# A mixture-of-experts layer on one core: the down product of a block one block later, up in one pass, and three waits placed anew

## What is computed

```python
hn = rmsnorm(h, g_ffn).reshape(B * L, D)
y = h + hier_moe(hn, ...).reshape(B, L, D)      # then the final rmsnorm

# hier_moe: the best of 4 groups, in it the best 2 of 4 experts, 16 experts in all
def expert_block(args):
    xb_i, e = args
    h = jax.nn.silu(xb_i @ w_gate[e]) * (xb_i @ w_up[e])
    return h @ w_down[e]
```

## Time and profile before

| | |
|---|---|
| Median of 3 runs | 1982.25 us (1982.22 to 1984.65) |
| Profiled execution | 1982.03 us |
| Its span, first to last instruction | 1980.3 us |
| Mean granted TensorE clock over the span | 0.972 of full speed |
| TensorE busy in the span | 95% |
| Start of the first x transposes of phase three | 1208.0 us |

### The profile page before, as it was taken

The page is one execution under the profiler, slowest core; times in us unless marked ns, Lnnn a source line. Parts: engine busy times, 40 slices in busy tenths (PEclk is TensorE's granted clock), DMA queues, the critical chain, the costliest instruction groups (busy, mean ns, idle before and its releaser), DMA issues. The chain is left out here.

```text
span 1980.3 us, 29050 instructions
## 1 busy us (share of the span) xinstructions
PE 1882.3 (95%) x10232; PEld 1606.3 (81%) x10233; DVE 1061.0 (54%) x2070; ACT 735.3 (37%) x1393; POOL 414.7 (21%) x571
## 2 busy tenths in 40 slices
PE   7899999999999999999999955999999999999996
PEld 5899987788888788888888844888888888888885
DVE  5634343545444554455453335566677666665572
ACT  4332323333334333333333213444455444444351
POOL 2000000000201001000001014444444434434453
PEclk9899999999999999999999956999999999999998
DMA  6222233422335223333222425577678857655552
GB/s 226 87 86 86 86 131 107 155 85 86 98 137 201 76 95 98 127 128 107 88 100 90 170 87 196 193 284 254 224 249 291 295 202 256 222 198 200 193 178 92
DMA packets 166568, 309.98 MB, mean 157 GB/s; under 512 B 18448, under 2 KB 85008, under 8 KB 166490
## 3 DMA queue, kind: packets, MB, share of 16 engines
q1 hardware_dynamic: 133706, 223.61, 32.8%
q0 software_dynamic: 32784, 85.33, 12.4%
HBM read 256.13 MB, written 83.69 MB: 172 GB/s over the span
## 5 line engine op out<-in xcount | busy, mean ns | idle before, releaser
L64 PE MATMUL bank<-xT_hi,wh 128*128 128x512 f32 (+1 forms) x960 | 339.8, 354 | 7.3 <-ACT S L751 5.4
L65 PE MATMUL bank<-xT_lo,wh 128*128 128x512 f32 (+1 forms) x960 | 339.1, 353 | 0.0
L66 PE MATMUL bank<-xT_hi,wl 128*128 128x512 f32 (+1 forms) x960 | 338.2, 352 | 0.0
L799 DVE TENSOR_TENSOR wl<-raw,wh 128x512 fp32r<-128x512 f32 x352 | 219.5, 685 | 201.3 <-ACT wh L602 201.2
L1783 PE MATMUL bank<-gu_hi,ex_hi 128*128 128x256 f32 (+1 forms) x960 | 314.1, 327 | 5.0 <-DVE ex_lo L1655 4.7
L1784 PE MATMUL bank<-gu_lo,ex_hi 128*128 128x256 f32 (+1 forms) x960 | 306.7, 319 | 0.0
L1785 PE MATMUL bank<-gu_hi,ex_lo 128*128 128x256 f32 (+1 forms) x960 | 306.6, 319 | 0.0
L602 ACT ACTIVATE wh<-raw 128x512 fp32r<-128x512 f32 x352 | 192.4, 620 | 84.6 <-PE bank L1223 54.7
L64 PEld LDWEIGHTS bank<-xT_hi,wh 128*128 128x128 f32 x960 | 181.5, 189 | 36.0 <-issue 9.8
L1783 PEld LDWEIGHTS bank<-gu_hi,ex_hi 128*128 128x128 f32 x960 | 182.8, 190 | 28.7 <-DVE gu_lo L1655 5.9
L66 PEld LDWEIGHTS bank<-xT_hi,wl 128*128 128x128 f32 x960 | 181.6, 189 | 25.3
(11 more groups left out here) (239 smaller groups left out, 3258.3 us busy)
## 6 DMA issues: line engine op xcount, KB each, us to landing
raw<-in_w_in SPq DMA_DIRECT2D x56, 1024.0 KB, 5.1
raw_gate_up<-in_w_gate SPq DMA_DIRECT2D x16, 2048.0 KB, 8.2
raw_gate_up<-in_w_up SPq DMA_DIRECT2D x16, 2048.0 KB, 10.1
raw_d<-in_w_down SPq DMA_DIRECT2D x16, 2048.0 KB, 9.9
raw<-in_w_out SPq DMA_DIRECT2D x16, 1024.0 KB, 6.3
raw<-in_w_up_pool SPq DMA_DIRECT2D x16, 512.0 KB, 3.5
raw<-in_w_up_gmlp SPq DMA_DIRECT2D x16, 512.0 KB, 4.5
h<-in_x_prompt SPq DMA_DIRECT2D x16, 512.0 KB, 5.0
```

The lines of the kernel that those rows point to most:

```text
L64: nc.tensor.matmul(out, lh, rh, start=(i == 0), stop=False)
L65: nc.tensor.matmul(out, lh, rl, start=False, stop=False)
L66: last = nc.tensor.matmul(out, ll, rh, start=False, stop=(i == n - 1))
L799: lo = lambda out, x, hi: tt(out, x, hi.bitcast(F32), ALU.subtract)
```

## The change

- On TensorE block j runs gate, up in one pass of 512 columns into one bank, the x transposes of the next block, then down of block j-1, then all four hidden transposes of block j into one bank. Block 0 has no down, and down of the last block stands behind the loops.
- In an expert's second block TensorE waits for the whole split of the down weights. ScalarE starts that split only when down of the expert before has ended (`y_done`), and both engines do it at the end of the first block.
- ScalarE copies hT_hi, and VectorE writes hT_lo, each in one instruction of 512 columns, at the head of the next block.
- VectorE writes the next rows' low parts directly behind `hid`, and `scale` comes behind them, in all blocks.
- `add` is one block later in the count and waits, besides, until the z stored before it has landed (`z_out`). GpSimd copies idx_y ahead of its own wait for `z_out`, so `scale` doesn't wait for the store.
- GpSimd carries the indices one step longer: one more copy per step (idx_1 to idx_2). At the end there is one more round of addition, root, h gather, scale and output store.

```diff
-    bankG, bankU, bankY = psum[0], psum[1:3], psum[3:5]
-    bankX, bankH = psum[5:7], [psum[7], psum[0]]
+    bankG, bankU, bankY = psum[0], psum[1], psum[3:5]
+    bankX, bankH = psum[5:7], psum[7]
...
                     wait_apart(pool, x_tr, j, passed_pool)
+                    nc.gpsimd.tensor_copy(idx_2[:, :], idx_1[:, :]).then_inc(moved_2, 1)
+                    wait_apart(pool, moved_2, j, passed_pool)
                     nc.gpsimd.tensor_copy(idx_1[:, :], idx[:, :]).then_inc(moved, 1)
...
                     out_landed(j)
-                    wait_apart(pool, z_out, 16 * j, passed_pool)
                     nc.gpsimd.tensor_copy(idx_y[:, :], idx_z[:, :]).then_inc(moved_y, 1)
                     wait_apart(pool, moved_y, j, passed_pool)
+                    wait_apart(pool, z_out, 16 * j, passed_pool)
...
+                def hidden_high(j):
+                    act.wait_ge(th_done, j + 2)
+                    nc.scalar.activation(hT[0][:, :, :], bankH[:, :].rearrange("p (k i) -> p k i", k=KH),
+                                         ACT.Copy).then_inc(hT_hi, 1)
...
                 def per_block(e, i, lo, j, first=False):
+                    hidden_high(j - 1)
                     if not first:
                         use_sigmoid_table(0)
                         square(j + 1)
                     act.wait_ge(g_done, j + 1)
                     nc.scalar.activation(sg[:, :], bankG[:, :], ACT.Sigmoid).then_inc(sg_ok, 1)
+                    rows_high(j + 2)
                     if first:
+                        act.wait_ge(down_in, 16 * i + 16)
+                        act.wait_ge(y_done, lo + 2)
+                        for k in range(KH):
+                            nc.scalar.activation(dn[0][:, k, :], raw_d[:, k, :], ACT.Copy).then_inc(e_hi, 1)
...
-                def add(n):
+                def add(n, stored):
 
                     dve.wait_ge(y_done, n)
                     dve.wait_ge(final_ok, n)
+                    if stored is not None:
+                        dve.wait_ge(z_out, 16 * stored)
                     dve.wait_ge(h_rows_in, 16 * n)
...
                     if not first:
+                        add(j + 1, j)
+                    hidden_low(j - 1)
+                    mean(j + 1)
                     dve.wait_ge(sg_ok, j + 1)
                     tt(sg[:, :], bankG[:, :], sg[:, :], ALU.mult)
                     dve.drain()
+                    dve.wait_ge(gu_done, j + 2)
+                    tt(hid[:, :], bankU[:, :], sg[:, :], ALU.mult).then_inc(hid_ok, 1)
+                    rows_low(2 * j + 3)
+                    scale(j + 1)
                     if first:
+                        for k in range(KH):
+                            dve.wait_ge(e_hi, SPLITS_ACT * i + 2 * KD + k)
+                            lo_half(dn[1][:, k, :], raw_d[:, k, :], dn[0][:, k, :]).then_inc(e_lo, 1)
...
+                def down(j):
+                    pe.wait_ge(z_ok, 2 * j + 4)
+                    pe.wait_ge(hT_lo, j + 2)
+                    for k in range(KH):
+                        for half in range(2):
+                            last = accumulate(bankY[half][:, :], hT, k, dn, k, slice(half * HALF, (half + 1) * HALF),
+                                              k, KH)
+                    last.then_inc(y_done, 1)
...
                     for k in range(KD):
                         pe.wait_ge(e_lo, SPLITS * i + KD + k + 1)
+                        last = accumulate(bankU[:, :], xT, k, gu, KD + k, slice(0, HALF), k, KD)
                     last.then_inc(gu_done, 1)
                     rows_of_x(16 * j + 32)
+                    if not first:
+                        pe.wait_ge(e_lo, SPLITS * i + SPLITS)
+                    if not begin:
+                        down(j - 1)
+                    hidden_transposed(j)
```

More of the change, by code:

```diff
@@ L1402, in phase_three @@
         idx_1 = sb("idx_1", [P, FIELDS], I32)
+        idx_2 = sb("idx_2", [P, FIELDS], I32)
         idx_h = sb("idx_h", [P, FIELDS], I32)
@@ L1486, in _ @@
                 nc.gpsimd.memset(half_neg[:, :], -0.5).then_inc(spare_ok, 1)
[L1487 to L1490, removed]
+                for tile in (idx_1, idx_h):
+                    nc.gpsimd.iota(tile[:, 0:1], pattern=[[0, 1]], base=SEQ + SAMPLE, channel_multiplier=1)\
+                        .then_inc(spare_ok, 1)
+                    nc.gpsimd.memset(tile[:, 1:2], 0).then_inc(spare_ok, 1)
+                    nc.gpsimd.memset(tile[:, 2:3], NOWHERE).then_inc(spare_ok, 1)
                 nc.gpsimd.memset(idx_y[:, :], NOWHERE).then_inc(spare_ok, 1)
@@ L1573, in _ @@
                 store_final(total)
[L1574 to L1579, removed]
+                for last, n in ((False, total + 1), (True, total + 2)):
+                    out_landed(n)
+                    wait_apart(pool, z_ok, 2 * n, passed_pool)
+                    nc.gpsimd.tensor_copy(idx_y[:, :], idx_h[:, :]).then_inc(moved_y, 1)
+                    root(n)
+                    wait_apart(pool, moved_y, n, passed_pool)
+                    if not last:
+                        next_h(n + 1, idx_1)
+                    store_final(n)
                 wait_apart(pool, x_rows_in, 16 * total + 16, passed_pool)
-                out_landed(total + 2)
+                out_landed(total + 3)
             @block.scalar
             def _(act):
-                act.wait_ge(spare_ok, 8)
+                act.wait_ge(spare_ok, 11)
                 act.wait_ge(tab_ok, 1)
@@ L1720, in split, with hidden_low @@
                         lo_half(gu[1][:, k, :], raw_gu[:, k, :], gu[0][:, k, :]).then_inc(e_lo, 1)
-                def hidden_low(c):
-                    lo_half(hT[1][:, 2 * c:2 * c + 2, :], bankH[c][:, 0:2 * P].rearrange("p (k i) -> p k i", k=2),
-                            hT[0][:, 2 * c:2 * c + 2, :]).then_inc(hT_lo, 1)
+                def hidden_low(j):
+                    dve.wait_ge(hT_hi, j + 2)
+                    lo_half(hT[1][:, :, :], bankH[:, :].rearrange("p (k i) -> p k i", k=KH), hT[0][:, :, :])\
+                        .then_inc(hT_lo, 1)
                 def per_block(e, i, lo, j, first=False):
-                    def down(k):
-                        if first:
-                            dve.wait_ge(e_hi, SPLITS_ACT * i + 2 * KD + k)
-                            lo_half(dn[1][:, k, :], raw_d[:, k, :], dn[0][:, k, :]).then_inc(e_lo, 1)
                     if not first:
-                        add(j + 1)
-                        mean(j + 1)
+                        add(j + 1, j)
+                    hidden_low(j - 1)
+                    mean(j + 1)
                     dve.wait_ge(sg_ok, j + 1)
@@ L1763, in _ @@
                 total = dve.value_load(blk_tab[0:1, 2 * NE - 1:2 * NE], min_val=1, max_val=MAXBLK)
-                add(total + 1)
-                mean(total + 1)
-                scale(total + 1)
+                hidden_low(total - 1)
+                for n in (total + 1, total + 2):
+                    add(n, total)
+                    mean(n)
+                    scale(n)
             @block.tensor
```

100 lines of the change are left out of this document (20 added, 80 removed).

## The result

The changed kernel takes 2040.11 us in the median of 4 runs (2038.14 to 2042.7), against 1983.45 us (1982.22 to 1985.8) for the kernel before: ratio 1.0287, 95% interval 1.0274 to 1.0299. It is 2.9% slower, where 1966 was forecast. The profiled execution took 2042.7 us, with a span of 2040.6 us and a mean granted clock of 0.955 (before 0.972).

A forecast was written before the change was run, and what follows sets the result against it. TensorE's work was taken to bound plain blocks, level with VectorE's weight splitting at expert changes. Blocks -38.5, gather waits +13 and ends +9.6 gave -15.9 us from 1982.03: forecast 1966 us, range 1951 to 1989.

The forecast's parts named there:

- A plain block: TensorE's block without a change of expert: 18.01 us becomes 17.70, bounds 17.6 and 17.9.
- An expert change: TensorE's block at a change of expert: no stall on the split weights, 17.85 us each, for 15 changes.
- The split's cast: VectorE's split of the weights at an expert change: starts 4.8 us after the x transposes, bounds 4.8 and 6.1.
- rival 2: At expert changes VectorE's split starts 6.1 us after the x transposes, 0.9 more for each of 15: 1980 us; chance 0.12.
- the sum: TensorE's stretch of 39 blocks, without the gather waits and the ends: 688.9 us against 727.4, 38.5 gained.
- The ends: First block and the added down, addition and output round after the last block: 9.6 us more in all.
- the term for the gather: TensorE's waits for x at experts' second blocks, gather beside the raw_d reload: 4 x 2.5 + 10 x 0.3 = 13 us.
- rival 3: The reload starves every gather: 3 us in up to 14 second blocks, 25 to 42 instead of 13, 1978 to 1995; chance 0.22.
- "fresh" experts: Experts whose GpSimd chain isn't late: store of z 7.6 us, gather 0.7 us ahead of the reload, wait 0.3 us.
- chained experts: Experts after a two-block one, GpSimd's chain late: gather starts 12.9 us after the first block's x transposes, wait 2.5 us.
- the sign of being wrong: At second blocks: the prediction is wrong if the x transposes wait in the experts with no late GpSimd chain too.
- Rival 1: The gather's packets pass beside the reload and no block waits: -38.5 + 9.6, so 1953 us; chance 0.20.

The follow-up runs named there:

- the best version: The changed kernel with GpSimd's gather of x ahead of its wait for the stored z, and the reload held until the needed gather landed: 1953.26 us, ratio 0.9844.

## Why the prediction was wrong

**Right.** A plain block was forecast at 17.70 and is 17.69 to 17.70. Up runs at 0.227 a matmul in one pass. The first interval is 14.06 (14.0). An expert change with no wait ahead of it is 17.73 (17.85). The split's cast at the change near 1850.71 starts 4.53 behind x-tr, where I chose +4.8 between 4.8 and 6.1; rival 2 didn't come:

```profile
1855.24 0.43 DVE L1713 CAST gu_hi<-raw_gate_up 128x512 fp32r<-128x512 f32 x1 [0.35 <-issue]
```

The reload starts at T+12.37 (T+12.4). The 39 blocks without waits and slow clock take 686.8, and in the best version 686.44, against the 688.9 of the sum. The last output is issued 24.5 behind the last x-tr (24), and the one TensorE wait on z_ok stands there, not in the loops:

```profile
2015.21 0.49 PE L1770 MATMUL bank<-dn_hi,hT_hi 128*128 128x512 f32 x1 [2.81 <-DVE z_rows L1698]
...
2029.99 0.98 POOL L1532 DMA_INDIRECT out<-final_rows,idx_y  x1 [0.30 <-issue]
```

The ends cost 13.0 instead of 9.6: 10.8 of it behind the last x-tr (9.9). The rest lies ahead of the first marked one, which comes anywhere from 1228.5 to 1232.7 in the kernels of this case; that part says nothing of the change.

**Wrong: the term for the gather, 13 us against 60.9 and 27.0.** The place was right, and the number of waits was that of rival 3 (up to 14). Three steps failed: the price of a gather, the ten experts without a real wait, and the clock that a wait costs.

First, the price of a gather beside the reload. I took 7.4 us from the earlier trace rows as if any gather in the reload's way cost that. But that gather started 3.9 us behind the reload's issue, and mine was to start 0.5 behind it. The reload of the earlier trace rows took 11.8 us to land, so the whole of this gather ran beside it. Its row stands first here. The second, which the prediction left out too, is the gather of another expert, 5.3 us behind its reload (1893.04 against 1887.74):

```profile
raw_d<-in_w_down SPq DMA_DIRECT2D x1, 2048.0 KB, 11.8
...
x_rows<-hn_rows,idx POOLq DMA_INDIRECT x1, 5.4
```

In the kernel before a gather takes less, give or take 0.3 us, the later it starts behind the reload: 7.4 us at 3.9, 6.7 at 4.5, 5.4 at 5.3, 4.7 at 6.4. Twelve of them started from T+9.4 to T+11.9 and all landed between T+16.2 and T+17.1. So 7.4 is no price for a start beside the reload's issue; it had to be more. In the changed kernel the 14 started from 0.3 ahead of the reload to 1.6 behind it, took 7.7 to 9.1 us, and landed at T+21.0 to T+22.6. I had T+20.3. They don't simply land with the reload either: in the changed kernel they land between 2.1 us ahead of it and 0.2 behind, in the kernel before between 0.5 ahead and 2.1 behind. Landings as far behind the reload's issue as the twelve (10.7 to 11.5 us) would have given T+23.1 to T+23.9. What sets the time exactly stays open.

Second, the "fresh" experts. I gave ten of 14 a wait of 0.3, since a store of 7.6 us would put their gather at T+11.7, 0.7 ahead of the reload. The difference was real in the kernel before: the store of z took 6.8 to 7.7 us after a three-block expert, 8.7 to 9.6 after a two-block one. In the changed kernel it took 9.0 to 9.6 in all 14. The load of up that runs beside it took 8.4 to 9.3 us in the fresh experts before and takes 11.7 to 13.0 in all 14 now; why, no run tells. The gathers started at T+12.0 to T+14.0, and the two at T+12.0, 0.3 ahead of the reload, still took 9.0. They are both in chained experts, so fresh ones were no better off. A margin of 0.7 us on worked-out times carried ten of the 14 terms. This was the sign of being wrong that I had named. Nor did the waits alternate: I had TensorE's delay let GpSimd catch up, but the store of z started at T-2.5 to T-0.4 in each of the 14.

Third, a wait costs more than its length. The sum had no term for the clock behind a standstill, and that is 27.0 us here.

The start that I worked out for a chained expert fits the expert at 1808.29, though it follows a three-block one and was fresh by my terms: the store at T-0.4 (T-0.7), its landing at T+8.7 (T+8.1), the gather 4.5 behind that (4.8), so T+13.2 (T+12.9). Two sums of the prediction are a little off, with no weight: T+20.3 less T+17.7 is 2.6, not 2.5, and the four parts of the later end of down(last) add up to 7.35, not 7.1.

**Rivals.** Rival 3 named the mechanism and put it at 25 to 42 us; with the wait as measured it is 14 x 4.4 = 62, and with the 27 of the clock 89. Rival 1's number, 1953, is that of the version with the early gather and the held reload, 1953.26, but not by its mechanism: there the gathers don't pass beside the reload, they land before it starts.

The Trainium skill, "DMA: Bandwidth & Descriptors" (Queues, rings and completion order), lets each DMA engine take turns between its queues by the packet. By that rule I had estimated 8.8 us for a late gather; the trace has 8.9 for the one shown and 7.7 to 9.1 for all 14, so for a gather that overlaps the load from its start the rule agrees. It was the better price of the two.

## What to carry to other kernels

When a change moves a large load, don't price a small transfer beside it by one that was seen at another distance from the load's start: 8.9 us at 0.8 behind it, 7.4 at 3.9, 4.7 at 6.4. A saving on the bounding engine is safe only if the inputs of its next step arrive earlier too: here the blocks got 1 us shorter, and the gather landed 5 us later behind T. Long entries in the list of waits on engines with slack (46.3 and 22.3 us here) may be worth 4 us, and a new wait of 4.4 us on the bounding engine may cost 6.3.

## What the runs showed of the hardware

- A 512 KB gather takes about twice its time beside a 2 MB load. Started 1.1 us ahead of the load it takes 4.4 to 5.1 us; 0.3 ahead or level, 8.9 to 9.0; 0.84 behind, 8.9; 3.9 behind, 7.4; 6.4 behind, 4.7. Another load of 2 MB (gate, 0.63 ahead of the gather) gives 9.1.
- Behind a standstill of 4.3 us TensorE, busy throughout, had a granted clock of 0.59 for 6.6 us, and of 1.00 after that. Behind the 13 others it was 0.54 to 0.79 over the same length. The 14 standstills cost 27.0 us on top of their 60.9. With matmuls in the gap the clock behind it was 1.00.
- Three copies of 128 x 3 integers on GpSimd, 0.2 us each elsewhere, took 0.93, 0.97 and 0.69 us while VectorE subtracted 128 x 1024 tiles (dn_lo). Where VectorE stood idle, in the kernel with extra matmuls ahead of T, they took 0.2.
